# A two-layer decoder trunk on one core: small products of 128 output rows cut into two of 64

## Time and profile before

| | us |
|---|---|
| median of 3 runs | 1997.93 (1996.48 to 2003.24) |
| span of the profiled execution | 1997.9 |
| TensorE matmul busy | 1830.2 (92%) |
| TensorE weight load busy | 1504.6 (75%) |
| VectorE busy | 1194.0 (60%) |
| ScalarE busy | 939.5 (47%) |
| mean granted TensorE clock | 0.949 |

### The profile page before, as it was taken

One profiled execution on the slowest core, in us unless ns is written; L12 is line 12 of the kernel. 1 busy time (PEld: TensorE's weight loads), 2 busy tenths in 40 slices (PEclk: granted clock), 3 DMA queues, 4 the chain that ended last, 5 costly groups with the idle time before them and its releaser, 6 DMA issues. The chain is left out here.

```text
span 1997.9 us, 26365 instructions
## 1 busy us (share of the span) xinstructions
PE 1830.2 (92%) x9764; PEld 1504.6 (75%) x9764; DVE 1194.0 (60%) x1766; ACT 939.5 (47%) x1288; POOL 321.8 (16%) x260
## 2 busy tenths in 40 slices
PE   8999999788999999889999947999999979999990
PEld 7888888686878888677877736788878858888770
DVE  4324543456655355669998855534344558999884
ACT  5112332453333332368888855222221138888880
POOL 0000000001000001234333310000001133443320
PEclk9999999868999999899999977999999989999995
DMA  5333434602000062589999974111215269999976
GB/s 205 133 121 121 129 105 124 131 1 85 1 1 1 7 214 101 193 310 369 372 371 371 346 273 148 42 52 49 88 48 199 99 265 351 382 380 369 367 287 262
DMA packets 145828, 373.16 MB, mean 187 GB/s; under 512 B 41014, under 2 KB 75966, under 8 KB 120974
## 3 DMA queue, kind: packets, MB, share of 16 engines
q1 hardware_dynamic: 114134, 308.34, 42.3%
q0 software_dynamic: 22368, 45.47, 6.3%
q10 hardware_dynamic: 9216, 17.93, 2.4%
HBM read 330.11 MB, written 75.10 MB: 203 GB/s over the span
## 5 line engine op out<-in xcount | busy, mean ns | idle before, releaser
L1522 PE MATMUL ex_ps_h<-even_split 128*128 128x512 f32 x768 | 194.5, 404 | 8.9 <-DVE even_split L1651 8.5
L1522 PE MATMUL ex_ps_h<-odd_split 128*128 128x512 f32 x768 | 194.8, 404 | 8.2 <-DVE odd_split L1651 7.9
L1522 PEld LDWEIGHTS ex_ps_h<-even_split 128*128 128x128 f32 x768 | 141.6, 191 | 47.9 <-DVE even_split L1651 14.6
L1522 PEld LDWEIGHTS ex_ps_h<-odd_split 128*128 128x128 f32 x768 | 141.6, 191 | 47.7 <-DVE odd_split L1651 14.1
L587 PE MATMUL in_ps<-in_w_hi,in_xT_hi 128*128 128x512 f32 (+1 forms) x440 | 170.4, 387 | 0.4 <-DVE in_xT_lo L465 0.3
L587 PE MATMUL in_ps<-in_w_lo,in_xT_hi 128*128 128x512 f32 (+1 forms) x440 | 166.9, 379 | 0.0
L587 PE MATMUL in_ps<-in_w_hi,in_xT_lo 128*128 128x512 f32 (+1 forms) x440 | 165.4, 376 | 0.0
L1919 PE MATMUL conv_ps<-conv_xT_hi,conv_w_hi 128*128 128x512 f32 x384 | 151.0, 393 | 1.9 <-DVE conv_w_lo L1856 1.9
L1919 PE MATMUL conv_ps<-conv_xT_lo,conv_w_hi 128*128 128x512 f32 x384 | 150.4, 392 | 0.0
L1919 PE MATMUL conv_ps<-conv_xT_hi,conv_w_lo 128*128 128x512 f32 x384 | 150.4, 392 | 0.0
L2658 ACT ACTIVATE att_prob<-att_ps_s 128x512 f32<-128x512 f32 x114 | 67.9, 596 | 154.5 <-PE att_ps_s L2593 154.4
(11 more groups left out here) (371 smaller groups left out, 4081.7 us busy)
## 6 DMA issues: line engine op xcount, KB each, us to landing
all_region<-in_moe_w_gate SPq DMA_DIRECT2D x16, 1024.0 KB, 9.8
all_region<-in_moe_w_up SPq DMA_DIRECT2D x16, 1024.0 KB, 18.9
all_region<-in_moe_w_down SPq DMA_DIRECT2D x16, 1024.0 KB, 14.1
experts_w_gu<-in_moe_w_gate SPq DMA_DIRECT2D x16, 1024.0 KB, 9.8
experts_w_gu<-in_moe_w_up SPq DMA_DIRECT2D x16, 1024.0 KB, 21.5
experts_w_d<-in_moe_w_down SPq DMA_DIRECT2D x16, 1024.0 KB, 16.5
slot_rows<-slots SPq DMA_DIRECT2D x32, 512.0 KB, 6.1
all_region<-in_ev_w_in SPq DMA_DIRECT2D x12, 1024.0 KB, 5.7
```

What stands on the lines that cost most here:

```text
L1522: last = pe.matmul(ps_h[:, u % 2, :], a[:, u % 2, k, :], w[:, k, :], start=(k == 0 and j == 0), stop=(k == KT - 1 and j == 2))
```

## The change

Each product named above is issued as two: the stationary operand's columns 0 to 63 give output rows 0 to 63, columns 64 to 127 give rows 64 to 127, in the same bank and the same columns. The moving operand is the same for both. Sums, waits and signals stay; the signal is still on the last product of the group.

```diff
+        half_tokens = (slice(0, P // 2), slice(P // 2, P))
 ...
                     for b in range(PAIRS):
                         for a in range(2):
                             h = 2 * b + a
-                            pe.matmul(ps_y[:, a, b * HD:(b + 1) * HD], scores[:, a, b, :],
-                                      qkv[:, c % 2, 2 * RET_W + h * HD:2 * RET_W + (h + 1) * HD],
-                                      start=(b == 0), stop=False, skip_group_check=True)
+                            for rows in half_tokens:
+                                pe.matmul(ps_y[rows, a, b * HD:(b + 1) * HD], scores[:, a, b, rows],
+                                          qkv[:, c % 2, 2 * RET_W + h * HD:2 * RET_W + (h + 1) * HD],
+                                          start=(b == 0), stop=False, skip_group_check=True)
 ...
-                            last = pe.matmul(ps_y[:, a, b * HD:(b + 1) * HD], qdT[at, b, :], state[at, b, :],
-                                             start=False, stop=(b == PAIRS - 1), skip_group_check=True)
+                            for rows in half_tokens:
+                                last = pe.matmul(ps_y[rows, a, b * HD:(b + 1) * HD], qdT[at, b, rows], state[at, b, :],
+                                                 start=False, stop=(b == PAIRS - 1), skip_group_check=True)
 ...
-                        last = pe.matmul(ps_l[:, t % 2, 0:NL], hT[:, t % 2, k, :], wr[:, k, :], start=(k == 0), stop=(k == KT - 1))
+                        for rows in half_tokens:
+                            last = pe.matmul(ps_l[rows, t % 2, 0:NL], hT[:, t % 2, k, rows], wr[:, k, :],
+                                             start=(k == 0), stop=(k == KT - 1))
 ...
-                        last = pe.matmul(ps_i, placed_at[:, c, t % 2, :], chosen[:, c, t % 2, :], start=(c == 0), stop=(c == 1))
+                        for rows in half_tokens:
+                            last = pe.matmul(ps_i[rows, :], placed_at[:, c, t % 2, rows], chosen[:, c, t % 2, :],
+                                             start=(c == 0), stop=(c == 1))
 ...
-                            last = pe_.matmul(ps_s[b % 2][:, t, h, :], keep.qT[0:QR, at * NH + h, :], keep.kcT[0:QR, h // R, :],
-                                              start=False, stop=True, skip_group_check=True)
+                            for rows in half_queries:
+                                last = pe_.matmul(ps_s[b % 2][rows, t, h, :], keep.qT[0:QR, at * NH + h, rows],
+                                                  keep.kcT[0:QR, h // R, :], start=False, stop=True, skip_group_check=True)
```

More of the change, by code:

```diff
@@ L2042, in prepare_attention @@
     N = BATCH * NH
+    half_queries = (slice(0, P // 2), slice(P // 2, P))
     with Pool_(nc, name) as m:
```

## The result

The changed kernel takes 1979.78 us (median of 4 runs, 1977.41 to 1981.82) against 1997.7 (4 runs): ratio 0.989 (95% interval 0.987 to 0.991). A second measurement, beside later runs, gives 0.988 (0.986 to 0.990). It is faster, as forecast, but by 22 to 24 us by the two ratios and not by 13.6: the ratio of the first measurement puts it at 1976 us on the scale of the median that the forecast started from, just under the range's lower end of 1977. The span of the profiled execution is 1975.8 us.

What follows compares the result with a forecast made beforehand. TensorE's own sequence bounds the projection with retention and both routes. Retention 3.9, router and lists 5.2, route tails 1.5 and compressed scores 3.0 sum to 13.6 us of 1997.9, so 1984.3 us; 8-in-10 range 1977 to 1993.

Steps and rivals of the forecast that it cites:

- the pitch of the products with the state: Retention's weighing: 16 pairs at 56 ns become 32 at 31 ns, 0.90 to 0.99 us a chunk.
- the compressed scores: Score stage before the attention: halved products shorten waits of the maximum and exponentials, 3.0 us saved, between 1 and 5.
- Reading pitches, not records: TensorE's small products: start-to-start pitch gives the cost, 108 ns whole, 31 ns in halves by turns as L613.
- rival (a): All halved products: loads of the two column halves wait for one another, 54 ns each; 10 us slower, 2008; chance 0.07.
- Rival (b): Retention's products with the state: quarter form stays at 56 ns; 6.4 us back, 1991; chance 0.07.
- The chain of waits: Compressed scores, batch by batch: first gains nothing, second's exponentials 2.3 us, third keeps the lead, fourth adds 0.8.
- the upper bound (5 us): Compressed scores: gain of 5 us if the shorter stretch gets the full clock sooner.
- Rival (c): Score stage to attention's start, and a route: clock falls or returns later with thinner products; about 1994; chance 0.13.
- The switch of form: TensorE, between whole and halved products: each change of form costs 0.16 us.
- The router's step: Routes' warm tiles: 1.79 us becomes 1.31, 0.48 x 14 = 6.7 us saved.
- the list's: Routes' warm tiles, lists' sums: 0.44 us becomes 0.57, a loss of 0.13 x 12 = 1.5 us.
- Rival (d): Routes: the gain turns into a wait for VectorE's placing chain; 5.2 us less gain, 1989.5; no separate chance given.

Runs made afterwards that it cites:

- e7: Changed kernel with the router's two column halves issued one after the other instead of by turns; 1989.24 us (one run).
- e2: Kernel before with only the products with the state (contraction 64) halved; ratio to before 0.9985 (0.9969 to 1.0001).
- e3: Kernel before with only the compressed scores' products halved; ratio to before 0.9961 (0.9947 to 0.9976).
- e5: Changed kernel with the lists' sums whole again, everything else halved; ratio to before 0.9891 (0.9871 to 0.9911).
- e8: Changed kernel with the router's products in four of 32 output rows; 1977.21 us (one run).
- e9: Changed kernel with the router in four of 32 rows and the lists' products 12 large products later; 1968.71 us, ratio to before 0.9832.
- e10: Changed kernel with 20 useless products filling TensorE's gap between second and third batch of compressed scores; 1977.17 us, ratio to before 0.9882.

## Why the prediction was right or wrong

The direction and the mechanism were right. The forecast gain was 9.5 us too small against the profile, mostly by two terms of the sum: the pitch of the products with the state, and the compressed scores.

**Reading pitches, not records: right.** L627 30 ns for 31, the router's run 0.90 us for 0.96, 0.53 us a tile less where 0.48 was forecast. L613 was a true sample of the form, eight times over. The slower rival (a) fell: e7 and the changed kernel issue the same 32 pairs of the router, differ only in how the two column halves take turns, and have 52 and 29 ns. The Trainium skill (TensorE: Matmul & The Clock Gate, Part 3, The mechanism) says that a load overlaps a matmul in flight only when its row group differs; these two runs go against it. e7 shows what (a) would have been: with the overlap taken away by the order, the router gains nothing.

**The state's products: the first mis-sized term.** I took 31 ns and called 27 the lower bound, because the next pair could not come sooner than L613's loads. That bound was a property of two parts of the array. With contraction halves and output halves there are four, and the pitch is 15 (e2, with nothing else changed). 32 x (31 - 15) = 0.5 us a chunk, 4.1 us in all, is most of the 4.6 by which this stage beat its forecast. Rival (b), no gain from quarters, was further off in the same place: I had set the doubt on the wrong side.

**The clock in the compressed scores: the second.** The chain of waits came as worked out, up to the third batch: counted from the first mask product, the second batch's exponentials began 2.5 us earlier, where 2.3 was forecast, and the third's 3.0. For the fourth I allowed 0.8 more. It came 6.9 us earlier. From 413 us on the clock was full, so that the products of the weighing and the next scores ran at full speed; no run divides this from the shorter products themselves. I had named it as the upper bound (5 us) and had not taken it; it was passed. Rival (c) had the right place and the wrong sign: shorter work went with a shorter half clock (e3, the scores alone: the same 10 us and 6.8 us less). Its reading of the clock was also a tile late. The clock fell at 404 us, with the third tile, which took 3.52 us like the fourth. Why it came back sooner with halved products stays open.

**The switch of form and the routes: right.** A pair of switches was put at 0.32 us. Measured as in the prediction, with the pitches taken off, the router's halves have 0.33 and the lists' 0.32: 0.09 on entry (0.32 instead of 0.23) and the rest on leaving. WEIGH has 0.46 on three. The router's step is 0.53 us shorter (0.48 forecast), the list's 0.10 longer (0.13 forecast), and the wait below takes 0.14 in five tiles: 0.53 x 14 - 0.10 x 12 - 0.14 x 5 = 5.5 us, where 5.7 was measured. That the changed kernel loses nothing against one with whole lists (e5) has another reason: whole ones would have lost their head start.

**Rival (d): right in its place, small in its price.** I had argued against it with DVE's 55%. But the wait is not for DVE's capacity but for one step of its chain, placing, whose lead over the list's products had been 0.39 us in the first route and 0.65 in the second. e7, whose router is about as long as the old one, has the lead back (0.65 and 0.91) and no wait. The wait took 0.14 us a tile in the first route and nearly all that e8 saved. My view of the waits of before showed nothing there, since a lead is not a wait.

**The total.** 8.5 + 6.9 + 5.7 + 2.0 = 23.1 us in the touched stages of one pair of profiles, against 13.6. The two stages of the mis-sized terms, 4.6 and 3.9 us beyond their forecasts, make up 8.5 of the 9.5 us of difference.

## What to carry to other kernels

A product with few streamed columns costs its weight load (here 106 and 108 ns a pair with 36 and 64 columns). Cut the stationary operand so that consecutive products go to different parts of the array, and alternate the parts: the same number of instructions cost 52 ns a pair one half after the other, 29 by turns and 9 in four by turns (twice as many). After shortening a step, look for the lead, not the wait: the next producer in line (here DVE's placing) was 0.39 us ahead in the first route. The second cut, into quarters, saved 0.36 us of the router's run there and nothing of the tile (e8), until the consumer was moved by twelve products in the order (e9, 0.72 us a tile).

## What the runs showed of the hardware that was not expected

- Four quarters of 64 rows and 64 columns take a pair every 15 ns on average at the full clock, four column quarters of 32 a pair every 9 ns (64 pairs in 0.77 us). At one column a cycle, which is what a large product's 0.23 us for 512 columns comes near, streams of 64 or 36 columns last 27 or 15 ns at 2.4 GHz; they must then overlap too. Why L2365, 64 output rows by turns and 128 columns, stays at 55 ns was not tested.
- TensorE was busy for 21.00 of 21 us in the records while its granted clock was 0.51, so a full busy row does not say that the clock is full. Shorter products, with more idle time between them, went together with a shorter half clock (10 us instead of 20 or 31), and the filled gap with none in its stretch (e10).
